# Bit-reversed places: where an expert's tokens stand among the 128 partitions of its gathered tile

## The chip, the core and the metric

The kernel runs on one core of a Trainium2 chip. The metric is the device time of one execution in microseconds (us). The engines are TensorE (PE, with its weight loads as PEld), VectorE (DVE), ScalarE (ACT), GpSimd (POOL) and SyncE (SP). SP issues nearly all plain transfers, POOL issues the indirect ones, and all of them are carried out by the core's 16 DMA engines.

## What is computed

A transformer layer over 1024 tokens of 1024 channels: a modulated RMS norm, a hybrid mixer, a second modulated norm, a mixture of experts, and a final norm. Only the mixture matters here:

```python
experts = gidx * EXPERTS_PER_GROUP + local          # two of 32 experts for each token
weights = top_p / jnp.sum(top_p, axis=-1, keepdims=True)
flat_e = experts.reshape(A)                         # A = 2048 assignments
order = jnp.argsort(flat_e)                         # an expert's tokens, in any order
def expert_block(args):
    xb, e = args
    return (jax.nn.silu(xb @ w1[e]) * (xb @ w3[e])) @ w2[e]
out = jnp.einsum('nk,nkd->nd', weights, y_assign)
```

An expert's rows are independent of each other, so the result does not depend on which row of a tile a token stands in.

Followed through on the reference's own inputs, the router gives the 32 experts these counts of tokens (2048 in all): 41 19 77 42 57 36 73 81 73 51 99 91 34 63 119 68 58 59 28 66 63 64 41 55 56 96 69 121 50 81 81 36.

## The kernel before

Everything is float32. The first part (to about 500 us) is the mixer, the router and the making of the lists; the expert stage runs from there to about 1045 us; then the two results of each token are read back, combined, normed and stored.

The expert stage has 24 passes of one 128-row tile each (`passes`, L52 to L58). Experts 0, 1, 2 come first, as they are; the other 29 are ranked by count. The first 16 ranks ("singles") have a pass of their own with up to 128 tokens. The last 16 ("couples", 8 of them) share a tile: one expert has places 0 to 63, the other places 64 to 127. Pass by pass the counts are 41, 19, 77, 121, (64, 51), 119, (63, 50), 99, 96, (63, 42), 91, (59, 41), 81, 81, (58, 36), 81, (57, 36), 73, 73, (56, 34), 69, (55, 28), 68, 66. A place without a token has an index out of bounds, for which no row is moved.

A place is a partition of the tile. DVE's `place` (L1843) compares each token's number in its expert's list (`pos_k`, counted over all tokens by PE's `places`, L1020) with the row `col_row`, which holds 0, 1, ... 127 in every partition (written by POOL at L652); L1854 gives a one-hot row, and PE's `listing` (L1032) sums one-hot rows and assignment numbers into `list_f`, one row of 128 places for each expert. L1086 to L1089 turn the rows into columns, one for each pass; for the couples they take the first 64 places of both experts. So `slot_i` and `slot_tok` hold, for each partition of each pass, which assignment and which token it is.

For each pass POOL issues two indirect DMAs: `gather` (L707, issued at L711), which reads each place's 4 KB row of the normed tokens from DRAM into that partition, and `scatter` (L715, issued at L719), which writes each place's 4 KB result row to the assignment's row in DRAM. Gather i+2 is issued when PE has transposed tile i; scatter i when DVE has evacuated pass i (L1986). 2048 rows of 4 KB are gathered and 2048 scattered in all.

The experts' weights, 96 units of 2 MB, stream through 8 slots in the fixed order of `stream` (L62 to L70: w1 of pass i, w2 of pass i-1, w3 of pass i). SP issues each unit (`load_unit`, L542, at L548) when the unit that had its slot was used up by PE. A unit has landed when all 16 DMA engines have brought their shares. For a single, ACT casts each up-projection's weights to a high part (`weight_hi`, L1421) and DVE makes the low part (`weight_lo`, L1975), PE then multiplies three times (L1114, L1117, L1120); couples are multiplied directly (L1125), as are the down-projections (L1144, L1150). PE's order is fixed: w1 of pass i, transposes of pass i-1's hidden rows and of tile i+1 (L1095), w2 of pass i-1, w3 of pass i.

The list that goes to DRAM for experts with more tokens than places (`index`, L1857) uses `pos_k` and not the place. No expert here has more than its tile holds.

Of the kernel before, what the change touches and what calls it, by code (L numbers as in the profile page):

```python
# [6 lines left out]
ALU = mybir.AluOpType  # L7
# [6 lines left out]
P = 128  # L14
# [5 lines left out]
def build(nc, x, c, w_ada, b_ada, g_norm1, g_norm2, w_in, w_out, gmlp_ln_g, gmlp_ln_b, gmlp_ws, gmlp_bs,  # L20
# [14 lines left out]
    E = exp_w1.shape[1]  # L35
# [6 lines left out]
    HALF = cap // 2  # L42
# [7 lines left out]
    FIXED, WIDE, COUPLES = 3, 16, 8  # L50
# [3 lines left out]
    for q in range(COUPLES):  # L54

        a, b = [4 + (WIDE - 4) * n // COUPLES for n in (q, q + 1)]
        passes += [(WIDE + q, WIDE + COUPLES + q)] + singles[a:b]
    PASSES = len(passes)  # L58
# [62 lines left out]
    with ExitStack() as ctx:  # L121
        def sb(name, shape, dt=F32):
            return ctx.enter_context(nc.sbuf_tensor(name, shape, dt))[:]
# [21 lines left out]
        ranked = sb("ranked", [E, E])  # L145
# [151 lines left out]
        col_row = R.take(P)  # L297
# [40 lines left out]
        list_f = M.take(P)[0:E, :]  # L338
# [22 lines left out]
        bank = [ctx.enter_context(nc.psum_tensor(f"bank{i}", [P, 512], F32)) for i in range(8)]  # L361
# [260 lines left out]
        def _(gp):  # L622
# [5 lines left out]
                             channel_multiplier=1)  # L628
# [9 lines left out]
            for h in range(2):  # L638
# [10 lines left out]
            gp.iota(tie_row, pattern=[[-1, E]], base=E - 1, channel_multiplier=0, allow_small_or_imprecise_dtypes=True)  # L649
            gp.memset(wide_cap, float(HALF))  # L650
            gp.iota(rank_row, pattern=[[1, E]], base=0, channel_multiplier=0, allow_small_or_imprecise_dtypes=True)
            gp.iota(col_row, pattern=[[1, P]], base=0, channel_multiplier=0, allow_small_or_imprecise_dtypes=True)  # L652
            gp.iota(aid_f.rearrange("p t k -> p (t k)"), pattern=[[2 * P, TILES], [1, 2]], base=-NONE, channel_multiplier=2,
                    allow_small_or_imprecise_dtypes=True)
            gp.iota(aid, pattern=[[2 * P, TILES], [1, 2]], base=0, channel_multiplier=2)
# [79 lines left out]
            with gp.If(most > 0):  # L735
                gp.iota(bidx.rearrange("p a b -> p (a b)"), pattern=[[1, OVER], [0, E]], base=0, channel_multiplier=0,
                        allow_small_or_imprecise_dtypes=True)
                gp.iota(nb, pattern=[[1, OVER]], base=0, channel_multiplier=0,
                        allow_small_or_imprecise_dtypes=True).then_inc(S["ov_iota"], 1)
# [21 lines left out]
        def _(pe):  # L761
# [279 lines left out]
            for t in range(TILES):  # L1041
# [19 lines left out]
                if t % 2 == 0 and t >= 4:  # L1061
# [20 lines left out]
                      stop=True).then_inc(S["order_mm"], 1)  # L1082
# [1 line left out]

            pe.wait_ge(S["slots_ready"], 1)
            pe.matmul(bank[7][:, FIXED:WIDE], list_f, ranked[:, FIXED:WIDE], start=True, stop=True)  # L1086
            pe.matmul(bank[7][0:HALF, WIDE:PASSES], list_f[:, 0:HALF], ranked[:, WIDE:WIDE + COUPLES], start=True, stop=True)
            pe.matmul(bank[7][HALF:P, WIDE:PASSES], list_f[:, 0:HALF], ranked[:, WIDE + COUPLES:E], start=True,
                      stop=True).then_inc(S["slots_mm"], 1)  # L1089

            def x_turn(buf, ready, n, done):
# [83 lines left out]
            with pe.If(most > 0):  # L1175
                pe.sem_inc(S["ov_y"], 1)
                with pe.Fori(0, OVER) as b:
# [13 lines left out]
                    for j in range(2):  # L1191
                        for k in range(KF):
                            mm = pe.matmul(bank[5 + j][:], hT_sb[:, k, :], down_of(7)[:, k, j * 512:(j + 1) * 512],
                                           start=(k == 0), stop=(k == KF - 1))
# [4 lines left out]
            for n, t in enumerate(by_pe):  # L1199
# [3 lines left out]
                for h in range(2):  # L1203
                    for k in range(2):
                        mm = pe.matmul(bank[2 * (n % 2) + h][:], w_diag[:, n, k, :], yy[:, t, k * D + h * HT:k * D + (h + 1) * HT],
                                       start=(k == 0), stop=(k == 1))
# [262 lines left out]
        def _(dve):  # L1469
            TT, TS, STT = dve.tensor_tensor, dve.tensor_scalar, dve.scalar_tensor_tensor  # L1470

            def mean_sq(src, dst, n, done):
                TS(dst, src, 1.0 / n, EPS, ALU.mult, ALU.add).then_inc(done, 1)  # L1473

            for f in range(2):
                dve.memset(zT[:, f, 0:2], 0.0)
            dve.memset(state[0].rearrange("p a b -> p (a b)"), 0.0)
# [81 lines left out]
            def gate_c(b):  # L1559
                _, _, f, h = blocks[b]  # L1560
                z = zT[:, f, 2 + h * HT:2 + (h + 1) * HT]
                dve.wait_ge(S["ev_act"], taken[b - 2])
                dve.wait_ge(S["blk"], b + 1)
                TT(z, z, bank[b % 2][:], ALU.mult).then_inc(S["ev_dve"], 1)
# [14 lines left out]
            def gate_b(b):  # L1579
                _, _, f, h = blocks[b]  # L1580
                dve.wait_ge(S["blk"], b + 1)
                TT(by_half(6 + f, h), by_half(6 + f, h), by_tile(bank[b % 2][:]), ALU.mult).then_inc(S["ev_dve"], 1)  # L1582
# [35 lines left out]
            two = lambda v: v.rearrange("p (t c) -> p t c", t=2)  # L1618
# [94 lines left out]
            for b in range(U0, BLOCKS + 2):  # L1713
# [17 lines left out]
                if b - 1 in mix_after:  # L1731
                    n = mix_after[b - 1]
# [4 lines left out]
                if 0 <= j < 2 * TILES:  # L1737
                    n, half_ = og_order[j]
# [338 lines left out]
            for t in range(TILES):  # L2077
                if t in by_pe:
                    n = by_pe.index(t)
# [46 lines left out]
```

## Time and profile before

| | |
|---|---|
| time, median of 3 runs | 1092.22 us (1091.91 to 1094.1) |
| span of the profiled execution | 1092.7 us |
| PE busy | 987.7 us, 90% |
| DVE, ACT, POOL busy | 545.4, 353.4, 127.2 us |
| DMA | 295.82 MB, mean 271 GB/s |
| granted TensorE clock, mean | 0.960 |

The profile is one execution; times in it count from its first instruction. The page cuts the span into 40 slices of 27.3 us and gives for each the busy share of an engine in tenths, the share of time in which the 16 DMA engines were busy, and what they moved. Other views list groups of instructions, who waited for whom, the chain of work that ended last, and the busy time in stretches of one's choice.

### The profile page before, as it was taken

To read this page: it belongs to the slowest core of one execution; us is meant where nothing else is said; L and a number is where in the kernel's file an instruction comes from. 1 tells how busy PE (TensorE), PEld (TensorE's weight loads), DVE (VectorE), ACT (ScalarE), POOL (GpSimd) and SP (SyncE) were. 2 spreads that over 40 slices of the span, in tenths; PEclk is the share of its full clock that TensorE was granted. 3 is DMA by queue.
4 is the path that set the end of the run, shared out by engine and by line. 5 is a ranking of instruction groups with operands and counts; after the bars stand their busy time and mean duration, and the time that the engine had idled before them with its cause. 6 is when DMAs were issued, how large, how long until landed. Compare 5 with 4: busy or idle time off the path is not lost.

```text
span 1092.7 us, 12936 instructions
## 1 busy us (share of the span) xinstructions
PE 987.7 (90%) x5014; PEld 676.3 (62%) x5014; DVE 545.4 (50%) x850; ACT 353.4 (32%) x525; POOL 127.2 (12%) x131
## 2 busy tenths in 40 slices
PE   3799999999999999975999999999899989988853
PEld 2477888888889688864675546454545355445521
DVE  2588643514653456555864536343634264334526
ACT  5521025322222443333652234222513233224112
POOL 2000000001210002212030221020100111010102
PEclk9899899999999999975999999999999999999977
DMA  9829511111303373358999999999999999998555
GB/s 369 297 93 340 202 40 39 39 39 40 117 1 136 116 273 97 113 194 219 335 366 369 417 426 427 427 426 425 427 428 426 427 426 411 423 423 361 227 241 230
DMA packets 52319, 295.82 MB, mean 271 GB/s; under 512 B 10889, under 2 KB 23194, under 8 KB 35874
## 3 DMA queue, kind: packets, MB, share of 16 engines
q1 hardware_dynamic: 43682, 274.00, 63.7%
q0 software_dynamic: 7424, 16.80, 4.0%
q10 hardware_dynamic: 1152, 4.19, 0.9%
q8 instruction: 40, 0.66, 0.2%
q14 instruction: 21, 0.17, 0.0%
HBM read 278.03 MB, written 25.33 MB: 278 GB/s over the span
## 4 chain that ended last, share of the span: by engine, by line
PE 66%; DMA 17%; DVE 8%; ACT 3%; issue 2%; DVEq 1%; POOL 1%; ACTq 0%; SPq 0%; POOLq 0%
DMA place_dt_float<-in_exp_w_dram 14%; PE bank L1144 7%; PE bank L1125 7%; PE bank L1120 4%; PE bank L823 4%; PE bank L818 4%; DVE place_dt_float32r L1975 4%; PE bank L820 4%; PE bank L819 4%; PE bank L824 3%; PE bank L825 3%; PE bank L1114 3%; PE bank L1117 3%; PE bank L992 2%; PE bank L995 2%
## 5 line engine op out<-in xcount | busy, mean ns | idle before, releaser
L1975 DVE TENSOR_TENSOR place_dt_float32r<-place_dt_float,place_dt_float32r 128x4096 fp32r<-128x4096 f32 x32 | 141.4, 4419 | 72.6 <-ACT place_dt_float32r L1421 72.6
L1421 ACT CAST place_dt_float32r<-place_dt_float 128x4096 fp32r<-128x4096 f32 x32 | 115.6, 3613 | 168.9 <-DMA place_dt_float<-in_exp_w_dram 147.2
L1144 PE MATMUL bank<-place_dt_float,arena 128*128 128x512 f32 x256 | 115.4, 604 | 1.7 <-issue 1.7
L1125 PE MATMUL bank<-place_dt_float,tail_dt_float 128*64 128x512 f32 x512 | 113.4, 595 | 2.3 <-DMA place_dt_float<-in_exp_w_dram 2.3
L719 POOL DMA_INDIRECT y_dram<-arena,slot_i x24 | 54.1, 2253 | 442.3 <-DVE arena L1986 442.3
L823 PE MATMUL bank<-low_r 128*128 128x256 f32 (+1 forms) x320 | 93.7, 293 | 0.0
L825 PE MATMUL bank<-low_r 128*128 128x256 f32 (+1 forms) x320 | 90.8, 284 | 0.0
L824 PE MATMUL bank<-low_r 128*128 128x256 f32 (+1 forms) x320 | 90.7, 284 | 0.0
L1114 PE MATMUL bank<-place_dt_float32r,tail_dt_float32r 128*128 128x512 f32 x256 | 70.3, 417 | 15.7 <-ACT place_dt_float32r L1421 12.8
L1144 PEld LDWEIGHTS bank<-place_dt_float,arena 128*128 128x128 f32 x256 | 47.9, 192 | 58.0 <-issue 56.7
L818 PE MATMUL bank<-low_r 128*128 128x512 f32 x192 | 78.5, 409 | 4.8 <-DVE arena L1582 3.6
L1125 PEld LDWEIGHTS bank<-place_dt_float,tail_dt_float 128*64 128x64 f32 x512 | 36.2, 137 | 74.4 <-issue 74.4
L636 POOL TENSOR_TENSOR stats<-stats,half 128x1 f32<-128x1 f32 (+1 forms) x34 | 26.3, 774 | 464.6 <-DVE stats L1473 437.8
L819 PE MATMUL bank<-low_r 128*128 128x512 f32 x192 | 76.5, 398 | 0.0
L820 PE MATMUL bank<-low_r 128*128 128x512 f32 x192 | 76.3, 397 | 0.0
L1114 PEld LDWEIGHTS bank<-place_dt_float32r,tail_dt_float32r 128*128 128x128 f32 x256 | 47.5, 192 | 42.9 <-issue 30.9
L1120 PE MATMUL bank<-place_dt_float32r,tail_dt_float32r 128*128 128x512 f32 x256 | 65.3, 397 | 8.2 <-DVE place_dt_float32r L1975 8.1
L1980 DVE COPY arena<-bank 128x512 f32<-128x512 f32 x24 | 16.6, 692 | 107.8 <-PE bank L1133 107.8
L1117 PE MATMUL bank<-place_dt_float32r,tail_dt_float32r 128*128 128x512 f32 x256 | 63.3, 389 | 0.0
L823 PEld LDWEIGHTS bank<-low_r 128*128 128x128 f32 x320 | 60.9, 190 | 3.4 <-issue 2.7
L1430 ACT ACTIVATE arena<-bank 128x512 f32<-128x512 f32 x24 | 14.3, 595 | 149.6 <-PE bank L1125 128.9
L1120 PEld LDWEIGHTS bank<-place_dt_float32r,tail_dt_float32r 128*128 128x128 f32 x256 | 46.9, 188 | 23.6 <-DVE place_dt_float32r L1975 14.1
(271 smaller groups left out, 1546.7 us busy)
## 6 DMA issues: line engine op xcount, KB each, us to landing
place_dt_float<-in_exp_w_dram SPq DMA_DIRECT2D x96, 2048.0 KB, 28.6
arena<-in_w_ada_dram SPq DMA_DIRECT2D x24, 1024.0 KB, 9.1
low<-in_w_in_dram SPq DMA_DIRECT2D x11, 1024.0 KB, 5.5
arena<-y_dram SPq DMA_DIRECT2D x8, 1024.0 KB, 7.4
arena<-in_x_dram SPq DMA_DIRECT2D x2, 2048.0 KB, 7.8
wout_dt_float<-in_w_out_dram SPq DMA_DIRECT2D x2, 2048.0 KB, 7.9
arena<-in_x_dram SPq DMA_DIRECT2D x8, 512.0 KB, 3.5
x_dram<-arena SPq DMA_DIRECT2D x8, 512.0 KB, 3.5
```

The lines of the kernel that those rows point to most:

```text
L818: pe.matmul(out_[:], hi[:, k, f_], hT_hi[:, k, t_], start=first, stop=False)
L819: pe.matmul(out_[:], lo[:, k, f_], hT_hi[:, k, t_], start=False, stop=False)
L820: mm = pe.matmul(out_[:], hi[:, k, f_], hT_lo[:, k, t_], start=False, stop=last)
L823: pe.matmul(w, hT_hi[:, k, t_], hi[:, k, :], start=first, stop=False)
L824: pe.matmul(w, hT_hi[:, k, t_], lo[:, k, :], start=False, stop=False)
L825: mm = pe.matmul(w, hT_lo[:, k, t_], hi[:, k, :], start=False, stop=last)
L1114: pe.matmul(out_[:], by_k(x_hi[i % 2])[:, k, :], hi[:, k, :], start=(k == 0), stop=False)
L1120: mm = pe.matmul(out_[:], by_k(x_hi[i % 2])[:, k, :], lo[:, k, :], start=False, stop=(k == KD - 1))
L1125: mm = pe.matmul(out_[rows_, :], x[:, k, rows_], w[:, k, :], start=(k == 0), stop=(k == KD - 1))
L1144: mm = pe.matmul(bank[5 + j][:], hT_sb[:, k, :], ws[0][:, k, cols], start=(k == 0), stop=(k == KF - 1))
L1421: act.copy(part_hi[0 if kind == "w1" else 1], alias[F32][n % SLOTS]).then_inc(S["w_hi"], 1)
L1975: TT(alias[F32R][n], alias[F32][n], part_hi[j].bitcast(F32), ALU.subtract).then_inc(S["w_lo"], 1)
```

## The change

`col_row` no longer holds 0, 1, ... 127 but, in column c, the number c with its seven bits reversed. A token whose number is n therefore takes place rev7(n): numbers 0, 1, 2, 3, 4 take places 0, 64, 32, 96, 16. The row is now made by DVE at the start of its stream (one memset and seven doublings, each with a drain), and POOL's iota is gone. The first 64 numbers of a list are those with even places, so the couples take the even places of a list (`first_half`, a view with a step of two): number n stands at place rev7(n)/2 of its half, which is n with six bits reversed. Singles take all 128 places.

```diff
-            gp.iota(col_row, pattern=[[1, P]], base=0, channel_multiplier=0, allow_small_or_imprecise_dtypes=True)
...
-            pe.matmul(bank[7][0:HALF, WIDE:PASSES], list_f[:, 0:HALF], ranked[:, WIDE:WIDE + COUPLES], start=True, stop=True)
-            pe.matmul(bank[7][HALF:P, WIDE:PASSES], list_f[:, 0:HALF], ranked[:, WIDE + COUPLES:E], start=True,
+            first_half = list_f.rearrange("p (n two) -> p two n", two=2)[:, 0, :]
+            pe.matmul(bank[7][0:HALF, WIDE:PASSES], first_half, ranked[:, WIDE:WIDE + COUPLES], start=True, stop=True)
+            pe.matmul(bank[7][HALF:P, WIDE:PASSES], first_half, ranked[:, WIDE + COUPLES:E], start=True,
                       stop=True).then_inc(S["slots_mm"], 1)
...
+            dve.memset(col_row[:, 0:1], 0.0)
+            dve.drain()
+            for n in (1 << b for b in range(7)):
+                TS(col_row[:, n:2 * n], col_row[:, 0:n], float(P // (2 * n)), None, ALU.add)
+                dve.drain()
```

## Rows read from the trace of the kernel before

**Rows 1.** The page: DMA share in tenths and GB/s by slice, and POOL's queue.

```profile
DMA  9829511111303373358999999999999999998555
GB/s 369 297 93 340 202 40 39 39 39 40 117 1 136 116 273 97 113 194 219 335 366 369 417 426 427 427 426 425 427 428 426 427 426 411 423 423 361 227 241 230
...
q0 software_dynamic: 7424, 16.80, 4.0%
```

**Rows 2.** Busy time in stretches of the expert stage; columns on the first line.

```profile
core 0: us, PE busy (x) PEld busy (x) DVE busy (x) ACT busy (x) POOL busy (x), PEclk, DMA share, GB/s
613.00:748.00 135.00, 134.74 (x582) 74.01 (x581) 61.51 (x64) 40.17 (x45) 22.16 (x12) 1.00 1.01 425
...
748.00:1018.00 270.00, 247.75 (x1041) 134.67 (x1040) 119.44 (x113) 84.35 (x78) 32.25 (x22) 1.00 0.99 417
...
910.00:937.00 27.00, 27.00 (x108) 13.02 (x109) 6.96 (x12) 3.47 (x7) 3.69 (x4) 1.00 0.98 412
```

**Rows 3.** Waits in 505:1050: engine, line, what for, us in total, times, longest.

```profile
ACT place_dt_float32r L1421 <- DMA place_dt_float<-in_exp_w_dram: 147.2, 17, 13.6
```

**Rows 4.** The chain that ended last, its end: start us, us, what.

```profile
964.05 7.04 PE bank L1125 x32
971.11 30.37 DMA place_dt_float<-in_exp_w_dram
1001.50 3.61 ACT place_dt_float32r L1421
1005.13 3.06 DVE place_dt_float32r L1975
...
1016.28 2.12 PE bank L1120 x8
1019.70 7.11 PE bank L1144 x16
...
1045.61 3.19 DMA y_dram<-arena,slot_i
```

**Rows 5.** Weight loads (L548) issued in 500:600, 600:650, 650:700 and 950:1000, in this order.

```profile
DMA to landing us min/median/max: 8.1/10.5/18.5
...
DMA to landing us min/median/max: 10.5/15.4/18.3
...
DMA to landing us min/median/max: 17.0/21.6/25.8
...
DMA to landing us min/median/max: 28.5/32.5/34.1
```

**Rows 6.** The last two weight loads (L548 in 987:990).

```profile
L548 SPq DMA_DIRECT2D place_dt_float<-in_exp_w_dram x2: 333/357/381, 988.0 to 988.4; - x2
...
DMA to landing us min/median/max: 28.5/31.2/33.9
```

**Rows 7.** Busy time in short stretches at the end of the weight stream, columns as before.

```profile
1000.00:1002.00 2.00, 2.00 (x12) 0.79 (x10) 0.00 (x0) 0.50 (x1) 0.00 (x0) 1.00 0.63 262
...
1002.00:1006.00 4.00, 3.17 (x15) 1.36 (x12) 0.86 (x1) 4.00 (x4) 0.00 (x0) 1.00 0.56 238
```

**Rows 8.** Timeline 996:1050: start, us, engine, line, operation, [idle before it].

```profile
1001.50 3.60 ACT L1421 CAST place_dt_float32r<-place_dt_float 128x4096 fp32r<-128x4096 f32 x1 [12.26 <-DMA place_dt_float<-in_exp_w_dram]
...
1004.57 0.39 SPq L592 DMA_DIRECT2D arena<-x_dram  x1
```

**Rows 9.** POOL's timeline, 645:656.

```profile
648.26 4.34 POOL L719 DMA_INDIRECT y_dram<-arena,slot_i  x1 [18.96 <-DVE arena L1986]
652.90 1.02 POOL L711 DMA_INDIRECT arena<-xn_dram,slot_tok  x1 [0.30 <-issue]
```

**Rows 10.** The chain where the expert stage begins.

```profile
504.12 4.45 DMA arena<-xn_dram,slot_tok
508.57 0.05 issue
508.61 1.99 PE bank L1095 x8
```

**Rows 11.** Timelines of DVE and POOL in the prologue, and PE's L1087 at 505.

```profile
1.30 0.48 DVE L1478 MEMSET arena<- 128x512 f32 x1
13.94 0.17 DVE L1473 TENSOR_SCALAR stats<-stats 128x4 f32<-128x4 f32 x1 [12.15 <-ACTq L1219]
...
26.37 0.67 POOL L652 IOTA arena<- 128x128 f32 x1
...
505.29 0.27 PE L1087 MATMUL bank<-ranked,arena 32*64 32x8 f32 x1
```

## The prediction

> **What bounds the kernel now.** The change moves no work on any compute engine that takes time; what it alters is into which partitions rows are gathered and from which they are scattered. So the question is what the indirect DMAs cost, and for whom. I read the page's DMA lines first: from 628 us on the DMA engines move 425 to 428 GB/s, from 900 us on a little less, until the weights end [rows 1]. In 613 to 748 us both PE and the DMA engines are full; in 748 to 1018 PE is busy for 247.75 of 270 us and so idle for 22.25 us, while the DMA share is still 0.99 [rows 2]. The waits say who is late: ACT's cast of freshly landed weights waits 147.2 us for them [rows 3]. The chain says which landing counts: the load issued at 971.11 us lands 30.37 us later, at 1001.50, and from there cast, split and PE work follow each other to the last scatter at 1045.61 [rows 4]. So up to about 740 us PE sets the pace, and from there the landing of weights does.
>
> A landing is that of the slowest of 16 DMA engines, and the trace shows that the 16 are not equally far. The time from issue to landing grows from a median of 10.5 us to 32.5 us [rows 5]. At 427 GB/s a 2 MB unit takes 4.9 us, so 32.5 us is more than six units in the queue of the slowest engine. Yet at 1002 to 1006 us, when the last unit (issued at 988.4, landing at 988.4 + 33.9 = 1022.3 us [rows 6]) is still 16 us from its landing and a new transfer is issued only at 1004.57 [rows 8], the DMA share is 0.56 [rows 7]: 0.56 x 16 = 9 engines work and 7 have nothing left. Seven engines were at least 20 us ahead of the last one. That is the slack the change can reach.
>
> **The change: how uneven are the rows.** All weights are dealt evenly, so what sets engines apart must be the rows, if it is not something of their own. One row is 4096 bytes; one engine's rate is 427 / 16 = 26.7 GB/s [rows 1], so one row costs its engine 0.153 us. That prices a row at the rate of the weight stream; nothing in the trace shows a single row's packet apart. Which engine serves a partition no view shows. I count three ways of dealing, with the counts of the passes given above:
> - A: places 0 to 63 go to eight engines, 64 to 127 to the other eight, four neighbouring places to one engine, then the next (place p to engine 8 x (p div 64) + (p div 4) mod 8).
> - B: eight neighbouring places to one engine.
> - C: place p to engine p mod 16.
>
> The time in which lags add up begins near 650 us, where the landing time starts to climb (15.4, then 21.6 us [rows 5]); before, PE holds the issue back and a late engine catches up. Gathers of passes 9 to 23 and scatters of passes 5 to 21 fall between there and the last landing (scatter 5 is issued at 648.26, gather 9 at 652.90 [rows 9]). Rows moved in that time, most loaded engine first:
> - A before: 256 256 256 256 256 254 228 213 173 138 114 104 84 75 70 56 (mean 174). The reason is plain: a single with 81 tokens fills places 0 to 80, eight rows on each of eight engines and one row or four on five others.
> - A after: 221 down to 132. With reversed bits 81 tokens give 4 to 6 rows to each engine. The couples gain nothing (their halves stay on eight engines each, 8 rows at most before and after, and the fuller expert always on the same eight), which is why it is 221 and not 174.
> - B before 256, after 209; C before 199, after 256 (56 more).
>
> Now the test by the row at 1002 to 1006 us. An engine that is done there is (1022.3 - 1002) / 0.153 = 133 rows behind the fullest in load. A has six such engines (114 and less) and one more at 138 next to them, so 9 or 10 at work: 0.56 to 0.63, as measured [rows 7]. B (down to 126 71 22 9 0) has four, or five with the one just short (0.69 or more). C before has 155 as its least, 44 rows or 6.7 us, so none would be done before 1015 us and the share would be 1.00. The row decides for A, against C.
>
> The Trainium skill, "DMA: Bandwidth & Descriptors", section "The descriptor swizzle", gives exactly A for a 128-partition transfer issued by GpSimd; the same page's table of specifications speaks of eight partitions per engine as the convention, which could be read as B, and by that the gain would be 1.8 us more than in the sum. The share measured at the end of the stream agrees with the former.
>
> **The sum.**
> 1. Weight stream: the fullest engine has 256 - 221 = 35 rows less by the last landings, 35 x 0.153 = 5.4 us (starting the count at 600 or 700 us gives 37 or 33 rows: 5.7 or 5.0). The landing at 1001.50, on the chain, comes that much earlier. What is late next is PE: it must have done its work up to there 5.4 us sooner, and its idle time from 748 us on is 22.25 us [rows 2]. It is full in 910 to 937 us [rows 2], so it can be only as far ahead there as the landings before it were (24 rows, 3.7 us, by then), and wins the rest after. So the whole 5.4 us pass. After 1020 us PE runs to its end without weights to wait for, and shifts with it.
> 2. First gather: 504.12 to 508.57 us on the chain [rows 10], with PE idle. Its 41 tokens give 8 rows to the fullest engine before and 4 after: 4 x 0.153 = 0.6 us less. Bounds: 0 (if its 4.45 us are latency) and 1.2 (if a row alternates with as much of another transfer). I take 0.6, and let it pass: the issues of the PE-paced part shift with it, and with them the time when the stream fills.
> 3. Last scatter: on the chain, 3.19 us [rows 4]. 66 tokens: 8 rows before, 5 after, 0.5 us less. Bounds 0 and 0.5.
> 4. Other gathers and scatters: never on the chain; earlier landing frees nothing that anyone waits for. 0.
> 5. DVE's eight small instructions and drains in the prologue: DVE is idle from 1.78 to 13.94 us [rows 11]; at the 0.17 us of the small operation there, and as much for each drain, 8 x 0.34 = 2.7 us lie in this gap of 12.15 us. Without the gap they would cost at most that. POOL loses one of a row of overlapping iotas (0.67 us [rows 11]), and nobody waits there. 0.
> 6. The two L1087/L1088 matmuls read their stationary operand with a step of two: 0.27 us at 505.3 [rows 11], with PE idle until 508.61 [rows 10]. Even twice as long it is hidden, from 0 to 0.3 us at worst. 0.
>
> Sum: 5.4 + 0.6 + 0.5 = 6.5 us. The profiled span of 1092.7 us becomes 1086.2; the median of the runs is 0.5 us under that span, so 1092.2 - 6.5 = 1085.7 us.
>
> **The rivals.**
> - *Dealing B.* 47 rows less, 7.2 us, with 0.6 and 0.5: 1083.9 us. The share of 0.56 speaks against it, but if the last rows are slower than 0.153 us the test is weaker.
> - *PE takes half of it.* The idle PE time may be the latency of casts, splits and hand-overs after each landing, which stay, and what is left may lie where it doesn't meet the landings that move. Then some 2.7 us of the stream's gain pass: 1092.2 - 2.7 - 1.1 = 1088.4 us. For it: in 910 to 937 us PE is full [rows 2]. Against: the cast had waited 12.26 us when the weights landed at 1001.50 [rows 8].
> - *The engines lag by themselves.* If the ones behind are slow for a reason of their own, 35 rows less on them still count, but the fullest engine by rows need not be the last one; in the extreme nothing moves: 1092.2 us, same. Against: nine engines are behind at 1002 us, and eight with ninth following is what A gives. The Trainium skill, same page, section "Latency and other measured facts", says that engines 7 and 15 are usually slower than the others, with its cause given as a guess; that would be two engines late, not nine, and no view here shows engines one by one.
> - *Dealing C, slower.* If neighbouring places go to neighbouring engines in turn, reversed bits are the worst choice: the first eight numbers of a list all take places that are multiples of 16, one engine. The fullest engine gets 57 rows more, 8.7 us, the first gather has 8 rows on one engine in place of 3 (0.8 us) and the last scatter 8 in place of 5 (0.5 us): 1102.2 us. It decides as soon as a partition's engine follows the low bits of its number. The share of 0.56 speaks against it, as worked out.
> - *It does not do what it says.* If lists were gathered as before, the time would be the same; the diff leaves no way for that, as L1854 is the only reader of `col_row`. It goes with the 'same' case.
>
> **How the numbers follow.** A with the full sum (1085.7, itself 1084.5 to 1087): 0.66. B: 0.08. PE takes half: 0.10. Same (own lags, or nothing): 0.10. C, slower: 0.06. The range takes in B, A and the half: its low end is B's with 1.2 for the first gather and a little of the runs' scatter, 1082.5; its high end reaches past the half towards the same case, 1090.5. A measurement of this kernel can tell about 0.2%, 2.2 us, from no change: faster is below 1090.0. Faster: 0.66 + 0.08 + 0.09 = 0.83; same: 0.11; slower: 0.06.
>
> **What would show it.** In the profile after: (a) the landing time of the weights still climbs after 650 us, but to a maximum of about 28 to 30 us and not 34; (b) at the end of the stream the DMA share falls late and steeply: with the engines 221 to 132 rows, nobody is done more than 89 x 0.153 = 13.6 us before the last, so 16 to 20 us before the last landing the share is 1.00 and not 0.56; (c) the last weight lands near 1016 us and not 1022.3; (d) the first gather lands in 3.9 us or so, the last scatter in 2.7; (e) PE's idle time between 748 us and the last landing is some 5 us less, with equal busy time; (f) nothing changes in DVE's and POOL's prologue for others. Wrong would be: the share still 0.56 there (then the lag is not of the rows), a landing that comes earlier while the end does not (PE bound), or landing times over 35 us (C).

## The result

| | before | after |
|---|---|---|
| time, median | 1092.56 us (1091.91 to 1094.1, 4 runs) | 1087.27 us (1085.41 to 1088.14, 4 runs) |
| ratio | | 0.9947 (95% interval 0.9927 to 0.9967) |
| span of the profiled execution | 1092.7 us | 1083.6 us |

By the medians the change makes the kernel 5.3 us faster, by the ratio 5.8 us (3.6 to 8.0); the forecast was 6.5 us. The profiled execution of after was the fastest of its four runs (1085.41 us), so its span shows more than the runs do; how much of it is the change is worked out below.

The page of after, DMA share in tenths and GB/s by slice (a slice is 27.1 us long now, 27.3 us before), and POOL's queue; the lines that answer to [rows 1]:

```profile
DMA  9828611111203263369889999999999999999665
GB/s 368 290 108 317 228 41 40 39 39 40 96 23 137 97 279 110 98 187 243 326 340 359 408 428 424 429 426 426 428 424 425 428 429 426 426 427 427 256 253 223
...
q0 software_dynamic: 7424, 16.80, 4.0%
```

The same packets and bytes. But the full rate now holds to the 37th slice (426 427 427), which ends at 1002 us; before, the 37th slice had only 361 [rows 1].

Busy time in stretches of after (us, busy time of PE, PEld, DVE, ACT, POOL, then granted clock, DMA share, GB/s), to be set beside [rows 2] and [rows 7]:

```profile
613.00:748.00 135.00, 134.71 (x580) 73.50 (x579) 61.46 (x64) 40.17 (x45) 22.15 (x12) 1.00 1.01 427
748.00:1018.00 270.00, 252.58 (x1058) 137.55 (x1057) 124.58 (x115) 86.94 (x79) 31.94 (x22) 1.00 1.00 423
910.00:937.00 27.00, 27.00 (x112) 12.19 (x111) 7.57 (x10) 6.75 (x7) 4.06 (x4) 1.00 1.01 425
...
992.00:996.00 4.00, 4.00 (x22) 1.65 (x20) 0.00 (x0) 1.93 (x1) 0.00 (x0) 1.00 0.99 418
```

The last two weight loads of after and the issue of the next transfer, to be set beside [rows 6] and [rows 8]:

```profile
L548 SPq DMA_DIRECT2D place_dt_float<-in_exp_w_dram x2: 333/357/381, 980.9 to 981.4; - x2
DMA to landing us min/median/max: 27.8/30.1/32.4
...
997.53 0.39 SPq L592 DMA_DIRECT2D arena<-x_dram  x1
```

The last weights land at 981.4 + 32.4 = 1013.8 us. At 992 to 996 us, 18 to 22 us before that and with no other large transfer issued, the share is 0.99: all 16 engines still work. About as far from the last landing, at 1002 to 1006 us, seven of 16 were done before (0.56) [rows 7]. This is the change as the trace shows it.

The chain of after, its beginning in the stage and its end (start us, us, what), beside [rows 10] and [rows 4]:

```profile
502.18 3.80 DMA arena<-xn_dram,slot_tok
...
964.61 29.43 DMA place_dt_float<-in_exp_w_dram
994.07 3.61 ACT place_dt_float32r L1421
997.71 3.05 DVE place_dt_float32r L1981
...
1027.21 7.12 PE bank L1144 x16
1036.49 2.74 DMA y_dram<-arena,slot_i
```

Where the profiled 9.1 us come from: the first gather is issued 1.94 us earlier (504.12, now 502.18), which has nothing to do with the change; from there to the landing on the chain it takes 994.07 - 502.18 = 491.9 us in place of 1001.50 - 504.12 = 497.4, so 5.5 us less; from that landing to the issue of the last scatter 42.4 us in place of 44.1. Of these 1.7 us the last down-projection has all: PE's last 16 matmuls took 8.8 us before, in a stretch where the granted clock was 0.79 of full speed, and 7.12 now. The rows of before (PE's timeline and the stretch 1035 to 1043 us), and the stretch of the same work in after:

```profile
1034.63 8.80 PE L1144 MATMUL bank<-place_dt_float,arena 128*128 128x512 f32 x16 [0.83 <-issue]
1035.00:1043.00 8.00, 8.00 (x16) 3.25 (x14) 0.00 (x0) 0.00 (x0) 0.00 (x0) 0.79 0.01 2
```
```profile
1027.00:1034.00 7.00, 6.79 (x16) 2.96 (x16) 0.11 (x1) 0.00 (x0) 0.00 (x0) 1.00 0.01 2
```

This is no effect of the order of places. The natural order made by DVE (first experiment) has 42.4 us there, with 7.12 us for the last 16 matmuls; the third order (second experiment), which is balanced, has 44.1 us, with 8.82.

Last, the scatter takes 2.74 us in place of 3.19. But from its issue to the end of the span there are 47.1 us in both kernels (1092.7 - 1045.61 and 1083.6 - 1036.49), so what it won didn't reach the end in this pair. The three parts add up to the 9.1 us: 1.9 + 5.5 + 1.7. Only the 5.5 us can be put down to the change, in this pair of executions. The same kernel profiled once more (last experiment) takes 489.6 us from the first gather's issue to the landing on the chain (503.63 to 993.22), 7.8 us less than before. The runs' 5.8 us lies between.

### The profile page after: what moved, and what is told of

The parts are those of the page before. It is cut to its first block, busy times and chain, and to the rows that moved or that the text cites. A ratio compares the mean times of both kernels' runs of the same rounds, so it can differ in the third digit from the quotient of the medians.

```text
span 1083.6 us, 12951 instructions
## 1 busy us (share of the span) xinstructions
PE 986.1 (91%) x5014; PEld 675.8 (62%) x5014; DVE 546.8 (50%) x858; ACT 353.3 (33%) x525; POOL 127.5 (12%) x130
## 4 chain that ended last, share of the span: by engine, by line
PE 67%; DMA 17%; DVE 8%; ACT 3%; issue 2%; DVEq 1%; POOL 1%; ACTq 0%; SPq 0%; POOLq 0%
DMA place_dt_float<-in_exp_w_dram 13%; PE bank L1144 7%; PE bank L1125 7%; PE bank L1120 4%; PE bank L822 4%; PE bank L817 4%; PE bank L819 4%; PE bank L818 4%; PE bank L823 3%; PE bank L824 3%; PE bank L1114 3%; DVE place_dt_float32r L1981 3%; PE bank L1117 3%; PE bank L991 2%; PE bank L997 2%; PE bank L994 2%
## 5 line engine op out<-in xcount | busy, mean ns | idle before, releaser
L1986 DVE COPY arena<-bank 128x512 f32<-128x512 f32 x24 | 16.6, 692 | 110.0 <-PE bank L1133 110.0
L1120 PEld LDWEIGHTS bank<-place_dt_float32r,tail_dt_float32r 128*128 128x128 f32 x256 | 48.1, 192 | 22.0 <-DVE place_dt_float32r L1981 12.3
## 6 DMA issues: line engine op xcount, KB each, us to landing
place_dt_float<-in_exp_w_dram SPq DMA_DIRECT2D x96, 2048.0 KB, 26.8
arena<-in_x_dram SPq DMA_DIRECT2D x2, 2048.0 KB, 12.2
```

Source lines behind the costliest of these rows:

```text
L1120: mm = pe.matmul(out_[:], by_k(x_hi[i % 2])[:, k, :], lo[:, k, :], start=False, stop=(k == KD - 1))
```

## The experiments

The theory T1: rows cost the DMA engine that serves their partition 0.153 us each, engines are dealt by A, and the fullest engine sets the landing of weights. The rivals: the cost is that of the fullest engine, but engines are dealt by B (T2), a gain by any spreading (T3), a PE that takes over (T4), the mean load (T5), a fixed gain that has nothing to do with the number of rows (T6), and a cost or gain of the new instructions (T0).

**Natural order, made by DVE.** The changed kernel with places 0 to 127 in order:

```diff
-            for n in (1 << b for b in range(7)):
-                TS(col_row[:, n:2 * n], col_row[:, 0:n], float(P // (2 * n)), None, ALU.add)
+            for b, v in enumerate((1, 2, 4, 8, 16, 32, 64)):
+                n = 1 << b
+                TS(col_row[:, n:2 * n], col_row[:, 0:n], float(v), None, ALU.add)
...
-            first_half = list_f.rearrange("p (n two) -> p two n", two=2)[:, 0, :]
+            first_half = list_f[:, 0:HALF]
```

> The changed kernel with natural places: the row of place numbers is made by the same eight DVE instructions and drains, but holds 0 to 127 in order, and the couples take places 0 to 63 as before. Theory T1 (the gain is that of the rows on the fullest DMA engine, dealing A; the new instructions are hidden): 256 rows on the fullest engine as before, so the time of before, 1092.6 us within 1 us. Rival T0 (part of the gain or a cost lies in the new instructions and the missing iota, not in the order): a time 1 us or more away from before.

Measured: 1093.28 us against 1093.13 for before, ratio 1.0002 (0.9988 to 1.0016). T0 falls: the new instructions cost nothing that can be measured (at most about 1.7 us by the interval), and the gain is the order's. Its stretch 1002 to 1004 us and its last weight loads:

```profile
1002.00:1004.00 2.00, 2.00 (x12) 0.76 (x10) 0.00 (x0) 2.00 (x1) 0.00 (x0) 1.00 0.59 246
...
L548 SPq DMA_DIRECT2D place_dt_float<-in_exp_w_dram x2: 333/357/381, 988.2 to 988.7; - x2
DMA to landing us min/median/max: 28.5/31.1/33.7
```

The share is 0.59 and the last landing is at 1022.4 us, as before.

**Which dealing: a third order.** Balanced by A, not by B. For a couple the first 64 numbers now lie in places 0 to 31 and 64 to 95 of a list:

```diff
+            for b, v in enumerate((32, 16, 8, 4, 2, 64, 1)):
...
+            for a in range(4):
+                mm = pe.matmul(bank[7][32 * a:32 * (a + 1), WIDE:PASSES], list_f[:, a % 2 * HALF:a % 2 * HALF + 32],
+                               ranked[:, WIDE + a // 2 * COUPLES:WIDE + (a // 2 + 1) * COUPLES], start=True, stop=True)
+            mm.then_inc(S["slots_mm"], 1)
```

> A third order of places: bit 0 of a token's number sets bit 6 of its place, bits 1, 2, 3 set bits 4, 3, 2, and bit 6, the slowest, sets bit 5. Singles and couples use the same number of places as before. Rows on the fullest engine in the time when lags add up (before: 256): by dealing A 213, by dealing B (eight neighbouring places to an engine) 252, as eight of its engines get next to nothing of the singles. T1 (dealing A): 43 x 0.153 + 1.1 = 7.7 us under before, 1084.9. T2 (dealing B): 0.6 us from the stream and 0.5 at most from the ends, 1091.5 to 1092. T3 (any spreading of the places helps, whatever the engine): about the gain of the bit-reversed order, 5 us, 1087.3.

Measured: 1086.29 us, ratio 0.9943 (0.9926 to 0.9960), so 6.2 us under before (4.4 to 8.1). T1 said 7.7 and is inside, T2 said 0.6 to 1.1 and is outside. B falls. T3 (5 us) is inside too, so this run does not decide between T1 and T3. In the trace the full share lasts as with reversed bits, and here the last weights land at 1016.0 us:

```profile
996.00:1000.00 4.00, 3.73 (x19) 1.26 (x15) 0.14 (x1) 3.77 (x2) 0.00 (x0) 1.00 1.02 430
...
L548 SPq DMA_DIRECT2D place_dt_float<-in_exp_w_dram x2: 333/357/381, 983.2 to 983.7; - x2
DMA to landing us min/median/max: 27.6/30.0/32.3
```

**Fewer rows still on the fullest engine.** Two kernels; both let the fuller expert of every second couple take the upper half, by the order of ranks:

```diff
-            gp.iota(rank_row, pattern=[[1, E]], base=0, channel_multiplier=0, allow_small_or_imprecise_dtypes=True)
+            gp.iota(rank_row[:, 0:WIDE], pattern=[[1, WIDE]], base=0, channel_multiplier=0, allow_small_or_imprecise_dtypes=True)
+            gp.iota(rank_row[:, WIDE:WIDE + COUPLES], pattern=[[2, COUPLES // 2], [COUPLES + 1, 2]], base=WIDE,
+                    channel_multiplier=0, allow_small_or_imprecise_dtypes=True)
+            gp.iota(rank_row[:, WIDE + COUPLES:E], pattern=[[2, COUPLES // 2], [1 - COUPLES, 2]], base=WIDE + COUPLES,
+                    channel_multiplier=0, allow_small_or_imprecise_dtypes=True)
```

and the first of the two also adds 64, 32, 8, 4, 2, 16, 1 in the seven doublings, so that the four fast bits of a number pick the engine.

> The order fitted to dealing A: the four fastest bits of the number set the four bits of the place that pick the engine by dealing A (6, 4, 3, 2), and every second couple has its fuller expert in the upper half. Fullest engine 199 rows, 57 less than before and 22 less than with reversed bits. T1: 57 x 0.153 = 8.7 us and 1.1 at the ends, 1082.8 us, if PE's idle time (22 us in the stage) lets it pass. Rival T4 (PE takes over: the reversed bits have already got what can be had): within 1 us of the reversed bits, 1086.3 to 1088.3.

Measured: 1083.16 us, ratio 0.9913 (0.9892 to 0.9934): 9.5 us under before (7.2 to 11.8), where T1 said 9.8.

> The changed kernel, with every second couple's fuller expert in the upper half, nothing else. Fullest engine 208 rows by dealing A, 13 less than with reversed bits alone and 48 less than before. T1: 48 x 0.153 + 1.1 = 8.4 us under before, 1084.2; that is 2 us under the reversed bits. T4 (PE takes over): no gain over the reversed bits, 1087.3.

Measured: 1084.09 us, ratio 0.9927 (0.9901 to 0.9953): 8.0 us under before (5.1 to 10.8), where T1 said 8.4.

The first is outside what T4 and T3 allowed as they were written down (1086.3 to 1088.3 us, and one gain of 5 us for any spreading). But both start from the gain of the reversed bits, and that was 5.8 us in one comparison and 7.4 in another (last experiment), with intervals that reach 8.0 and 10.1 us. With that, the times alone don't exclude T3 or T4: the interval of the first kernel overlaps those of the reversed bits, that of the second still more. What excludes T3 is where each engine stands at the end (below). Against T4 speaks PE's idle time in the stretch of 748 to 1010 us: 21.6 us before, 16.6 with reversed bits, 12.9 with the fitted order (first line: before, second: the fitted order):

```profile
748.00:1010.00 262.00, 240.39 (x1012) 129.23 (x1011) 112.61 (x109) 81.19 (x77) 27.94 (x21) 1.00 0.99 417
```
```profile
748.00:1010.00 262.00, 249.06 (x1049) 135.94 (x1048) 121.47 (x115) 86.92 (x79) 32.27 (x22) 1.00 1.01 426
...
L548 SPq DMA_DIRECT2D place_dt_float<-in_exp_w_dram x2: 333/358/383, 977.4 to 977.8; - x2
DMA to landing us min/median/max: 27.6/29.9/32.3
```

The fitted order has the lowest time of this study. It beats before clearly; its lead over the changed kernel, 2.1 or 3.7 us depending on which of that kernel's two comparisons is taken, is not shown beyond the noise.

**The rows counted twice.** If rows on the fullest engine are what costs, twice the scatters must widen the gap between the orders. In natural order, in reversed order and in the fitted one:

```diff
...
                                       oob_is_err=False).then_inc(scat[i % 2], 16)
+                if i < PASSES - 1:
+                    gp.indirect_dma_start(out=y2_dram, out_offset=bass.IndirectOffsetOnAxis(ap=slot_i[:, c_:c_ + 1], axis=0),
+                                          in_=y_sb[i % 2], in_offset=None, bounds_check=2 * T - 1,
+                                          oob_is_err=False).then_inc(scat[i % 2], 16)
...
-                wait(dve, scat[i % 2], 16 * (i // 2))
+                wait(dve, scat[i % 2], 32 * (i // 2))
```

> The kernel before, with each scatter but the last issued a second time, into a second DRAM tensor that nobody reads: the same 4 KB rows from the same partitions once more, output unchanged. In the time when lags add up this puts 136 rows more on the fullest engine by dealing A (256 to 392) and 97 on the mean one. T1: at least 136 x 0.153 = 20.8 us over before, 1113.9 us (a few us more if the stretch bound by transfers begins earlier now). T5 (what counts is the mean load of the engines): 97 x 0.153 = 14.8 us, 1107.9.

Measured: 1119.97 us against 1093.22, ratio 1.0245 (1.0212 to 1.0278): 26.8 us over before (23.2 to 30.4). T5 (14.8 us) falls, also if the second scatters of all passes are counted: 124 rows on the mean engine, 19.0 us. T1's 20.8 was given as the least. The weight loads are late sooner here, which is the likely reason for the rest. Loads issued in 600:650, in 650:700 and the last two:

```profile
DMA to landing us min/median/max: 10.6/18.4/24.3
...
DMA to landing us min/median/max: 21.8/30.4/34.7
...
L549 SPq DMA_DIRECT2D place_dt_float<-in_exp_w_dram x2: 333/357/381, 1007.0 to 1007.5; - x2
DMA to landing us min/median/max: 30.7/33.6/36.4
```

Their median was 15.4 and 21.6 us before [rows 5]. If the rows count from two passes earlier on, 152 second scatters lie in the stretch, 23.3 us; between first gather and last landing this run takes 23.2 us longer than before (table below).

> The changed kernel with each scatter but the last issued twice, as in the run before. Fullest engine 341 rows against 392 in natural order with scatters twice: T1: 51 x 0.153 + 1.1 = 8.9 us under that run, 1105.0. T6 (the gain of the reversed bits is a fixed one, of the first gather and the ends or of when rows land): 5 to 6 us under that run, as without the second scatters.

Measured: 1107.32 us, ratio 1.0125 (1.0092 to 1.0159): 12.7 us under the natural order with scatters twice (by the ratios 13.1, with some 5 us to either side). T6 (5 to 6 us) falls; T1's 8.9 is too low as well, but within the noise.

> The order fitted to dealing A with alternating halves, and each scatter but the last issued twice. Fullest engine 308 rows, 84 less than in natural order with scatters twice. T1: 84 x 0.153 + 1.1 = 14.0 us under that run, 1099.9. T6: 9 to 10 us under it, as without the second scatters.

Measured: 1105.02 us, ratio 1.0099 (1.0068 to 1.0130): 15.0 us under the natural order with scatters twice, T1 said 14.0 and T6 9 to 10 (by the ratios 16.0, with some 5 us to either side, which leaves T6 just outside). Between these last two kernels there are 2.3 us where T1 has 5.0; with an interval of 3.4 to 3.7 us to either side of each time, the two runs fit T1's 5.0 and no difference at all.

> The changed kernel as it is, beside the others on the same chip: 5 to 6.5 us under before, 1087 us (T1 from its rows: 35 x 0.153 + 1.1 = 6.5).

Measured: 1085.54 us, ratio 0.9932 (0.9908 to 0.9956), 7.4 us under before (4.8 to 10.1).

**All runs by the trace.** The issue of the last weight load plus its time to landing, minus the issue of the first gather, leaves out what varies ahead of the stage. Rows are those on the fullest engine by dealing A, in the stretch of the prediction:

| kernel | rows | first gather to last landing, us | time against before |
|---|---|---|---|
| before | 256 | 518.2 | |
| natural order by DVE | 256 | 517.8 | +0.2 us |
| reversed, the change | 221 | 511.6, 509.4 | -5.8, -7.4 us |
| third order | 213 | 509.8 | -6.2 us |
| reversed, halves alternate | 208 | 509.2 | -8.0 us |
| fitted, halves alternate | 199 | 507.8 | -9.5 us |
| natural, scatters twice | 392 | 541.4 | +26.8 us |
| reversed, scatters twice | 341 | 529.8 | +13.7 us |
| fitted, scatters twice | 308 | 526.2 | +10.8 us |

(Times against before are the ratio times the median of before that was measured beside the run; the first gather is issued at 504.12, 504.63, 502.18 and 503.63, 506.15, 504.45, 502.27, 502.52, 501.50 and 502.09 us.) From 256 to 199 rows 10.4 us are won: 0.18 us for a row, 0.16 without the 1.2 us that the first gather lands earlier (below). That is the 0.153 us of the estimate and a little more. With scatters twice 15.2 us are won for 84 rows (0.18) and 11.6 us for 51 (0.23).

**Engine by engine.** The printed views show only the mean of the 16 engines. But the trace of each run has 16 landings for every weight load, one for each engine's share. Those of the last load say how far apart the engines are at the end. The rows of each dealing, at 0.153 us each, say how far apart they should be:

| kernel | first to last of the 16 landings, us | by A | by B | by C |
|---|---|---|---|---|
| before, natural order by DVE | 22.3, 22.1 | 30.6 | 39.2 | 6.7 |
| reversed, the change | 14.6, 14.5 | 13.6 | 9.5 | 37.8 |
| third order | 11.8 | 11.0 | 24.5 | 25.9 |
| reversed, halves alternate | 11.1 | 9.5 | 4.4 | 37.8 |
| fitted, halves alternate | 8.1 | 7.0 | 8.0 | 33.8 |
| natural, scatters twice | 24.7 | 45.9 | 60.0 | 10.3 |
| reversed, scatters twice | 21.2 | 20.7 | 14.4 | 57.7 |
| fitted, scatters twice | 12.5 | 10.9 | 12.2 | 51.3 |

Dealing A comes within 1.6 us in every balanced order. B does so in the fitted order alone and misses by 5 to 13 us elsewhere; C misses by 14 us and more. So T3 falls: how far apart the engines are goes by the engine that each place belongs to, and not by spreading as such. The natural orders show less than A gives, and the single landings say how. In before seven engines land the last load within 1.4 us of each other, at 1000.0 to 1001.4 us, then one at 1006.2, one at 1012.3 and seven at 1018.6 to 1022.3. That is A's grouping: 56 to 138 rows, 173, 213, and 228 to 256. But the first seven should be 12.5 us apart by their rows. They land together some 11.6 us after the issue at 988.4, and the last two units take 9.8 us at 4.9 each, so they had next to nothing else left. A lead ends where an engine runs out of issued loads.

The landings also bear on the little more than 0.153 us. By A six engines of before have 254 to 256 rows, yet the last of all lands 1.9 us after the next and 3.5 us after the sixth. So engines differ by some microseconds for a reason of their own, and single last landings carry that; whether it is the whole of the excess is not shown.

## Why the prediction was right

Step 1, the weight stream, was right in mechanism and near in size. 5.4 us were forecast. On the chain of the profiled pair it is 5.5 us including what the first gather gives (492 in place of 497 us), so 4.9 without it, and 7.8 and 6.7 in the repeated profile; by the table's last landings, with the first gather's share taken off, 6.0 us (518.2 - 511.6 - 0.6) and 7.7 us (518.2 - 509.4 - 1.1). The dealing A, taken from one share of 0.56, held against B in the second experiment, against C in the change itself (by C it had 57 rows more, and would have been slower), and against both in the landings engine by engine. The test that chose it was right in its count of seven, but not in its working for each engine: it took an engine's lead to be its missing rows times 0.153 us, and in before the leads stop at 22.3 us where A's rows give 30.6. For the slowest engine, which never runs out of loads, this makes no difference. The rival that engines lag by themselves falls too: with the fitted order, the last three engines land within 0.1 us of each other. The Trainium skill, "DMA: Bandwidth & Descriptors", section "The descriptor swizzle", gives A for a plain 128-partition transfer; these indirect ones follow it as well, by the second experiment's 6.2 us where B would give about 1, and by its 11.8 us between first and last landing where B gives 24.5.

That PE lets the gain pass was right: its idle time in 748 to 1018 us fell from 22.25 [rows 2] to 17.42 us, and it fell further with the fitted order. The rival that PE takes half of it had 3.8 us in all, which is inside the interval of the first comparison (3.6 to 8.0 us) and outside that of the second (4.8 to 10.1); the landing on the chain, earlier by 5.5 and 7.8 us, speaks against it.

Step 2, the first gather: it lands in 3.80 us in place of 4.45 [rows 10], 0.6 us as forecast; 3.38, 3.28, 3.20 and 3.12 us in other kernels with 4 rows at most on an engine, and 4.27 in the natural order by DVE. That it passes to the end was assumed; the runs don't show it apart from step 1. Step 3, the last scatter: it lands in 2.74 us in place of 3.19 [rows 4], as forecast. But the time from its issue to the end was 47.1 us in both kernels of the profiled pair, and 46.7 to 48.1 us in the other kernels with one scatter for each pass, so that its 0.5 us reach the end is not shown. The sum of 6.5 us came out near the 5.8 and 7.4 us of the runs, while single executions scatter by 2 us or more; that it is so close is in part luck.

Step 5, the instructions in the prologue. DVE's timeline of after, start, us, operation, beside [rows 11]:

```profile
0.86 0.06 DVE L1476 MEMSET arena<- 128x1 f32 x1 [0.86 <-PEq L2119]
1.00 1.84 DVE L1479 TENSOR_SCALAR arena<-arena 128x1 f32<-128x1 f32 x7
...
13.98 0.17 DVE L1473 TENSOR_SCALAR stats<-stats 128x4 f32<-128x4 f32 x1 [10.11 <-ACTq L1219]
```

They take 2.1 us (0.86 to 2.95), bound at 2.7, and lie in the gap as forecast. Step 6, the stride in the stationary operand: L1087 takes 0.27 us with it and without it, [rows 11] and after at 503.34.

One of the signs named ahead was wrong: the time from issue to landing should have risen to 28 to 30 us only, and it rose to 33.2 us (31.1 in the median, loads issued from 950 us on):

```profile
DMA to landing us min/median/max: 27.8/31.1/33.2
```

Before it was 34.1 [rows 5]. The reasoning had held the issue fixed. But SP issues a load when PE has used up the slot, and PE runs behind the landings: when the landings came 7 us earlier the issues did too (981.4 in place of 988.4 us). With eight slots full, this time is the depth of the queue, and not how far the slowest engine is behind; that is read from the share of the DMA engines while the last weights are under way. Likewise the last landing came at 1013.8 and not at 1016 us, of which 1.9 us lay ahead of the stage.

What stays open: whether the engines' own differences are all of what makes a row seem worth 0.16 to 0.23 us and not 0.153; whether it is the engine itself or something else that serves the same partitions that a row holds up; and whether the four or so microseconds by which the profiled executions differ ahead of the stage (first gather issued at 501.50 to 506.15 us) follow anything. That two executions of the same kernel differ by 2 us in first gather to last landing (511.6 and 509.4) is about as much as single steps of this series.

## What to carry to other kernels

A transfer is as late as the slowest of its 16 DMA engines (here 22.3 us behind the first), so small indirect transfers beside a saturating stream should be judged by the rows on their fullest engine. Where tiles are partly filled, deal the rows so that the number's fastest bits pick the engine; here that costs eight tiny instructions, 2.1 us in a gap where DVE was idle. And a DMA share well under 1.00 while somebody still waits for the last transfer says that the engines are uneven.

## What the runs showed of the hardware

- Partitions are dealt to DMA engines in fours, and 0 to 63 and 64 to 127 to different eights: orders that are balanced by this dealing and not by eights of neighbours win, 6.2 us (4.4 to 8.1), where the other dealing gives about 1. The 16 landings of a load are as far apart as its rows say: 11.8 us, where this dealing gives 11.0 and eights of neighbours 24.5.
- An engine's lead over the others ends where it has no issued loads left: in before seven engines land the last load within 1.4 us, although their rows differ by up to 82 (12.5 us).
- Second scatters of 4 KB rows cost 23.2 us in natural order, from first gather to last landing, for 136 rows more on the fullest engine, or 152 if they count from two passes earlier on.
- PE's granted clock can fall to its lower level, 1.2 GHz, within the last down-projection: 0.50 at 1036 to 1038 us in before, after two waits of 0.8 us each between short pieces of work. The 16 matmuls took 8.8 us with 0.79 granted in the stretch 1035 to 1043 and 7.12 us at 1.00. The third order has the same 1.7 us more; the change has the same two waits and no fall.
